# The prologue of a gated-linear-attention layer on one core: low-rank product and first unit begin with 288 tokens

## The chip, the cores and the metric

The kernel runs on one core of a Trainium2 chip. The metric is device microseconds of one execution. Three runs of the kernel before gave a median of 1057.85 us (1057.68 to 1058.1).

## What is computed

One decoder layer on 512 prompt tokens and 64 sample tokens (8 sequences of 8), 576 tokens of 1024 features. The layer normalizes x (RMS norm with a weight per feature), multiplies it by one wide input matrix, runs two gated linear recurrences (GLA and HGRN2) over slices of the product, merges them, projects them out, and runs a SwiGLU feed-forward network.

```python
def rms_norm(x, w):
    y = xf * lax.rsqrt(jnp.mean(xf * xf, axis=-1, keepdims=True) + EPS)
    return (y * w.astype(jnp.float32)).astype(x.dtype)
...
    proj = h @ w_in_l
    (gq, gk, gv, gg, glr, hq, hf, hi, hg, ga, gb) = jnp.split(proj, split_points, axis=-1)
    log_a = jax.nn.log_sigmoid((glr @ w_lr2_l + b_lr_l).astype(jnp.float32)) / GLA_TAU
...
            h = x + rms_norm(m, norm_mix_post[l])
            f = swiglu(rms_norm(h, norm_ffn_pre[l]), w_ffn_in[l], w_ffn_out[l])
            return h + rms_norm(f, norm_ffn_post[l])
```

The change touches only what happens to x before and during the first two products with `w_in`: those with the 16 columns `glr` and with the first 128 columns of `hf`.

## The kernel before

Every large product runs on TensorE in three passes over operands split in two: a value is a rounded main part (`x_hi`, `w_hi_t`) and a rest (`x_lo`, `w_lo_t`), and the passes are lo times hi, hi times lo and hi times hi. ScalarE makes main parts (a copy that rounds), VectorE makes rests (a subtraction). x is wanted with features on the 128 partitions, so each tile of 128 tokens is turned by 8 transposes of 128 by 128 on TensorE into PSUM, whence ScalarE and VectorE take main part and rest.

The tokens are five tiles: four of 128 (tiles 0 to 3) and one of 64 (tile 4, the sample tokens). The projections use two halves of 288 tokens (`HT`), so that the first half is tiles 0, 1 and the first 32 tokens of tile 2. Every engine has its program written out by hand, with semaphores between them; nothing is reordered.

The prologue, by engine:

- SyncE (SP, lines 433 to 441) issues the loads: the norm weight (`gain`, 4 KB), the five x tiles, the weights of the low-rank product (unit 0) and of the first unit (unit 1), 512 KB each, and then eight small ones. Later loads of weights wait for the splits of earlier ones.
- ScalarE (from line 555) loads its table, then for each tile takes squares and their sum (line 562), Ln (564) and Exp (566), which gives the inverse root; two tiles later it makes the main part of a turned tile (line 570). Then come the split of unit 2's weights (line 273, a helper) and the copy of the low-rank result.
- VectorE (from line 773) multiplies the identity with the norm weight into eight diagonal blocks (line 776), scales each tile by its inverse root and by the weight rows that stand in PSUM (line 783), and two tiles later subtracts for the rest (line 788). The rests are counted on the semaphore `x_lo_s`.
- TensorE (from line 1025) makes the weight rows by two matmuls of ones and the diagonal blocks (line 1029), turns the tiles (line 1039) with four dummy matmuls of ones and ones ahead of tiles 3 and 4 (line 1036), then makes the low-rank product for both halves (line 1046, 32 passes) and goes into the units: `unit_passes` (line 287) makes 48 passes of 288 columns for each.
- GpSimd (POOL, from line 472) splits the weights of units 0 and 1 into main part and rest, after which it builds masks (line 485 on) and, once all tiles are turned, loads states and copies the sample tokens into `x_both`.

The turned tiles go in turn to PSUM banks 0 and 1, 2 and 3, 4 and 5; the weight rows stand in banks 6 and 7; the low-rank product goes to banks 4 and 5, unit 1 to banks 2 and 3. These lines set the order on TensorE:

```python
        for c in range(NT):
            n = tok(c)
            if c >= 3:
                pe.wait_ge(x_lo_s, c - 2)
                for _ in range(4):
                    nc.tensor.matmul(ps[:, 3 * (c - 3), 0:P], ones[:, :], ones[:, :], start=True, stop=True)
            pe.wait_ge(scaled, c + 1)
            for k in range(KT):
                m = nc.tensor.transpose(turned_x(c)[:, k, :], xt[c][0:n, k * P:(k + 1) * P], ident[0:n, 0:n])
            m.then_inc(turned, 1)
        pe.wait_ge(w_lo, 2)
        for q in range(2):
            pe.wait_ge(x_lo_s, 3 if q == 0 else NT)
```

Of the kernel before, what the change touches and what calls it, by code (L numbers as in the profile page):

```python
# [63 lines left out]
V_BANK = {0: 2, 1: 3, 4: 4, 2: 0, 3: 1}  # L64
UB = 1 + G * NU
# [80 lines left out]
def build(nc, x_prompt, x_sample, state_gla, state_hgrn, norm_mix_pre, norm_mix_post, norm_ffn_pre,  # L146
# [53 lines left out]
    gain_diag = sem("gain_diag")  # L200
# [139 lines left out]
    gains = O[:, :, :].rearrange("p a b -> p (a b)")[:, 0:D].rearrange("p (k n) -> p k n", k=KT)  # L340
# [3 lines left out]
    def turned_x(c):  # L344
        return ps[:, 2 * (c % 3):2 * (c % 3) + 2, :].rearrange("p a b -> p (a b)").rearrange("p (k t) -> p k t", k=KT)[:, :, 0:tok(c)]

    def tokens(c):
        return slice(c * P, c * P + tok(c))

    square = v_t[:, :, :].rearrange("p a b -> p (a b)")[:, 0:D]  # L350
# [80 lines left out]
    @block.sync  # L431
    def _(sp):
        sp.dma_start(gain[:, 0, :], norm_mix_pre).then_inc(gain_in, 16)
        for c in range(NT):
            sp.dma_start(xt[c][0:tok(c), :], xp_v[c] if c < NC else xs_v).then_inc(x_in[c], 16)
        load_unit(sp, 0, win_v[:, :, GLR:GLR + P])
        load_unit(sp, 1, win_v[:, :, UNITS[0][0]:UNITS[0][0] + P])
        for t, v in ((gain[:, 1, :], hgrn_lb),
                     (onm[:, 0:2], gla_onorm), (onm[:, 2:3], hgrn_onorm), (blr4[:, :], gla_b_lr),
                     *((wlr4[i * GR:(i + 1) * GR, :], gla_w_lr2.rearrange("o r d -> (o r) d")) for i in range(4))):  # L440
            sp.dma_start(t, v).then_inc(small, 16)
        for j in range(G):
            for n, (col, width, t) in enumerate(UNITS):
                if j == 0 and n == 0:
                    continue
                u = j * NU + n + 1
                sp.wait_ge(w_lo, u)
                if col == "v":
                    load_values(sp, u, j, t)
                else:  # L450
                    first = j * width + col + t * P
                    load_unit(sp, u, win_v[:, :, first:first + P])
        for u in range(UB, UB + 5):
            sp.wait_ge(w_lo, u)
            load_out(sp, u)

    @block.gpsimd
    def _(pool):
# [84 lines left out]
        pool.wait_ge(x_hi_s, NT)  # L543
        nc.gpsimd.tensor_copy(x_both[:, :, 0:TS], x_hi[:, :, TP:T].bitcast(F32)).then_inc(both_s, 1)
        pool.wait_ge(x_lo_s, NT)
# [8 lines left out]
    def _(act):  # L554
        act.preload_act_table_set("natural_log_exp_and_others")

        act.wait_ge(setup, SETUP)
        for i in range(NT + 2):
            if i < NT:
                n = tok(i)  # L560
                act.wait_ge(x_in[i], 16)
                act.activation(square[0:n, :], xt[i][0:n, :], ACT.Square, accum_out=stat[0:n, 0, i:i + 1])
                act.drain()
                act.activation(stat[0:n, 1, i:i + 1], stat[0:n, 0, i:i + 1], ACT.Ln, scale=1.0 / D, bias=eps_c[0:n, :])
                act.drain()
                act.activation(stat[0:n, 1, i:i + 1], stat[0:n, 1, i:i + 1], ACT.Exp, scale=-0.5).then_inc(squared, 1)
            if i >= 2:
                c = i - 2
                act.wait_ge(turned, c + 1)
                act.activation(x_hi[:, :, tokens(c)], turned_x(c), ACT.Copy).then_inc(x_hi_s, 1)  # L570
# [193 lines left out]
    def _(dve):  # L764
# [9 lines left out]
        dve.wait_ge(consts, 5)  # L774
        dve.wait_ge(gain_in, 16)
# [3 lines left out]
        for i in range(NT + 2):  # L779
            if i < NT:  # L780
                n = tok(i)
                dve.wait_ge(squared, i + 1)
                dve.scalar_tensor_tensor(xt[i][0:n, :], xt[i][0:n, :], stat[0:n, 1, i:i + 1], gain_rows[0:n, :],
                                         ALU.mult, ALU.mult).then_inc(scaled, 1)
            if i >= 2:
                c = i - 2
                dve.wait_ge(x_hi_s, c + 1)
                dve.tensor_tensor(x_lo[:, :, tokens(c)], turned_x(c), x_hi[:, :, tokens(c)].bitcast(F32), ALU.subtract).then_inc(x_lo_s, 1)
# [236 lines left out]
    def _(pe):  # L1025
        pe.wait_ge(gain_diag, 1)
        pe.wait_ge(consts, 5)
        for k in range(2):
            m = nc.tensor.matmul(gain_rows[:, k * HALF:(k + 1) * HALF], ones[:, :], gains[:, 4 * k:4 * k + 4, :], start=True, stop=True)
        m.then_inc(gain_row, 1)  # L1030
        for c in range(NT):
            n = tok(c)
            if c >= 3:
                pe.wait_ge(x_lo_s, c - 2)
                for _ in range(4):
                    nc.tensor.matmul(ps[:, 3 * (c - 3), 0:P], ones[:, :], ones[:, :], start=True, stop=True)
# [4 lines left out]
        pe.wait_ge(w_lo, 2)  # L1041
        for q in range(2):
            pe.wait_ge(x_lo_s, 3 if q == 0 else NT)
# [4 lines left out]
        m.then_inc(unit_done, 1)  # L1048
# [134 lines left out]
        for j, n in SLOTS:  # L1183
            if j < G and V0 <= n < GATE0:
                value_unit(j, n - V0)
            elif j < G:
# [4 lines left out]
            elif n < 3:  # L1191
# [810 lines left out]
```

## Time and profile before

| | us |
|---|---|
| median of three runs | 1057.85 |
| the profiled execution | 1056.84 |
| its span, first to last instruction | 1055.1 |
| TensorE busy (matmuls) | 1040.6 (99%) |
| VectorE busy | 664.8 (63%) |
| ScalarE busy | 468.8 (44%) |
| GpSimd busy | 66.6 (6%) |
| first low-rank pass | 18.06 |
| first pass of unit 2 | 28.61 |

Times within the span are counted from its start. "SPq" and "POOLq" are instructions that issue a load or store; the load itself runs on the 16 DMA engines. A row of the timeline is a start, a duration, the engine, the line, the operation with output and inputs, and how many such instructions are merged into the row; in brackets stands the idle time before it and what ended it. Matmul rows overlap, so the distance of two starts says what one costs, and an f32 matmul has two records.

### The profile page before, as it was taken

How to read it: one execution, taken by the hardware profiler on the slowest of the kernel's cores; microseconds unless marked ns; L12 is line 12 of the kernel's file. 1: busy time of each engine (PE TensorE's matmuls, PEld its weight loads, DVE VectorE, ACT ScalarE, POOL GpSimd, SP SyncE). 2: the span in 40 equal slices, each digit the busy share in tenths (PEclk: the TensorE clock that was granted, in tenths of full speed). 3: DMA queues.
4: the chain of work that ended last, by engine and by line, in shares of the span. 5: the costliest groups of instructions: out<-in, count | busy, mean ns of one | idle time of the engine just before them, and what ended most of it. 6: DMA issues, size and time to landing. Idle time of an engine off the chain costs nothing.

```text
span 1055.1 us, 24326 instructions
## 1 busy us (share of the span) xinstructions
PE 1040.6 (99%) x10648; PEld 962.3 (91%) x10648; DVE 664.8 (63%) x974; ACT 468.8 (44%) x727; POOL 66.6 (6%) x86
## 2 busy tenths in 40 slices
PE   7999999999999999999999999999999999999997
PEld 5989999989999899999899878999999999888886
DVE  6266625676526756356765478888888888744544
ACT  6433344722445333446225547644444434633532
POOL 5200002100004000031000000000000000000000
PEclk9999999999999999999999999999999999999999
DMA  6522223622216332136232192133243242422212
GB/s 195 162 80 81 64 69 101 198 64 75 73 48 204 97 82 81 52 111 190 62 82 70 52 319 61 41 99 102 81 111 90 81 120 61 140 80 80 82 58 90
DMA packets 130777, 105.25 MB, mean 100 GB/s; under 512 B 4272, under 2 KB 115888, under 8 KB 130672
## 3 DMA queue, kind: packets, MB, share of 16 engines
q1 hardware_dynamic: 125808, 85.88, 28.3%
q0 software_dynamic: 4864, 17.83, 5.6%
q8 instruction: 84, 1.38, 0.5%
q14 instruction: 21, 0.17, 0.1%
HBM read 91.89 MB, written 11.80 MB: 98 GB/s over the span
## 4 chain that ended last, share of the span: by engine, by line
PE 94%; DVE 2%; ACT 1%; DMA 1%; ACTq 1%; issue 0%; DVEq 0%; SPq 0%
PE ps L287 34%; PE ps L1911 23%; PE ps L1935 13%; PE ps L1178 10%; PE ps L396 3%; PE ps L1080 2%; PE ps L1111 2%; PE ps L1101 1%; PE ps L1113 1%; PE ps L1118 1%; PE ps L1094 1%; PE ps L1150 1%; DVE h_t L937 1%; PE ps L1076 1%; PE ps L1138 0%; PE ps L1064 0%
## 5 line engine op out<-in xcount | busy, mean ns | idle before, releaser
L273 ACT ACTIVATE w_hi_t<-w_raw_t 128x1024 fp32r<-128x1024 f32 x73 | 77.2, 1058 | 302.1 <-PE ps L287 217.8
L287 PE MATMUL ps<-x_hi,w_lo_t 128*128 128x288 f32 x896 | 195.6, 300 | 0.0
L277 DVE TENSOR_TENSOR w_lo_t<-w_raw_t,w_hi_t 128x1024 fp32r<-128x1024 f32 x73 | 89.7, 1229 | 168.0 <-ACT w_hi_t L273 167.6
L287 PE MATMUL ps<-x_hi,w_hi_t 128*128 128x288 f32 x896 | 191.5, 295 | 0.0
L287 PE MATMUL ps<-x_lo,w_hi_t 128*128 128x288 f32 x896 | 191.0, 295 | 0.0
L287 PEld LDWEIGHTS ps<-x_hi,w_lo_t 128*128 128x128 f32 x896 | 143.0, 188 | 4.4 <-issue 2.5
L287 PEld LDWEIGHTS ps<-x_lo,w_hi_t 128*128 128x128 f32 x896 | 143.8, 188 | 0.0
L287 PEld LDWEIGHTS ps<-x_hi,w_hi_t 128*128 128x128 f32 x896 | 143.8, 188 | 0.0
L1911 PE MATMUL ps<-x_hi,w_lo_t 128*128 128x288 f32 x276 | 81.4, 295 | 0.6 <-issue 0.6
L1911 PE MATMUL ps<-x_lo,w_hi_t 128*128 128x288 f32 x276 | 81.3, 295 | 0.0
L1911 PE MATMUL ps<-x_hi,w_hi_t 128*128 128x288 f32 x276 | 81.3, 295 | 0.0
L1482 ACT ACTIVATE w_hi_t<-merged 128x1024 fp32r<-128x1024 f32 x35 | 37.0, 1057 | 57.4 <-PE ps L1911 57.4
L858 DVE TENSOR_TENSOR Q<-Q,B 128x768 f32<-128x768 f32 (+1 forms) x24 | 23.8, 992 | 58.8 <-PE ps L1080 23.8
L1935 PE MATMUL ps<-w_hi_t,x_hi 128*128 128x512 f32 x180 | 57.2, 390 | 0.0
L1911 PEld LDWEIGHTS ps<-x_hi,w_lo_t 128*128 128x128 f32 x276 | 51.8, 188 | 1.0 <-issue 1.0
L1722 DVE TENSOR_TENSOR work<-work,ps 128x288 f32<-128x288 f32 x100 | 45.1, 451 | 10.8 <-PE ps L1911 7.2
L1911 PEld LDWEIGHTS ps<-x_hi,w_hi_t 128*128 128x128 f32 x276 | 51.9, 188 | 0.0
L1911 PEld LDWEIGHTS ps<-x_lo,w_hi_t 128*128 128x128 f32 x276 | 51.8, 188 | 0.0
L1178 PE MATMUL ps<-w_lo_t,x_hi 128*128 128x512 f32 x128 | 51.3, 401 | 0.0
L1178 PE MATMUL ps<-w_hi_t,x_hi 128*128 128x512 f32 x128 | 50.0, 390 | 0.0
L1178 PE MATMUL ps<-w_hi_t,x_lo 128*128 128x512 f32 x128 | 49.8, 389 | 0.0
L1613 DVE TENSOR_TENSOR w_lo_t<-merged,w_hi_t 128x1024 fp32r<-128x1024 f32 x36 | 44.0, 1224 | 8.6 <-ACT w_hi_t L1482 8.6
(345 smaller groups left out, 2252.5 us busy)
## 6 DMA issues: line engine op xcount, KB each, us to landing
w_raw_t<-in_w_in_dram SPq DMA_DIRECT2D x57, 512.0 KB, 3.8
merged<-in_w_ffn_in_dram SPq DMA_DIRECT2D x22, 512.0 KB, 5.2
w_raw_t<-in_w_ffn_in_dram SPq DMA_DIRECT2D x22, 512.0 KB, 4.6
w_raw_t<-in_w_ffn_out_dram SPq DMA_DIRECT2D x22, 512.0 KB, 3.7
w_raw_t<-in_w_in_dram SPq DMA_DIRECT2D x32, 256.0 KB, 3.8
h_t<-in_x_prompt_dram SPq DMA_DIRECT2D x8, 512.0 KB, 5.0
h_t<-in_state_gla_dram POOLq DMA_DIRECT2D x4, 1024.0 KB, 6.4
h_t<-in_state_hgrn_dram POOLq DMA_DIRECT2D x8, 512.0 KB, 7.8
```

Source lines behind the costliest of these rows:

```text
L273: nc.scalar.activation(w_hi_t[:, u % NSPL, 0:nk, :], w_raw_t[:, u % NRAW, 0:nk, :], ACT.Copy).then_inc(w_hi, 1)
L277: nc.vector.tensor_tensor(w_lo_t[:, u % NSPL, 0:nk, :], w_raw_t[:, u % NRAW, 0:nk, :], w_hi_t[:, u % NSPL, 0:nk, :].bitcast(F32), ALU.subt ...
L287: m = nc.tensor.matmul(out[:, q, :], w[:, u % NSPL, k, :], x(k, q), start=first and i == 0, stop=last and i == len(todo) - 1)
L396: ins = pe.matmul(out_bank(half, c), x[:, k, cols], w[:, kk, :], start=first and i == 0, stop=last and i == len(todo) - 1, skip_group_chec ...
L858: dve.tensor_tensor(qf, qf, first.broadcast_to(shape), ALU.mult)
L1080: m = nc.tensor.matmul(s[t:t + STRIP, o + t // 2:o + (t + STRIP) // 2], K[:, h, c * C + t:c * C + t + STRIP], second(Q[:, h, c * C + t:c * ...
L1178: m = nc.tensor.matmul(ps[:, V_BANK[c], :], x, w, start=q == 0 and t == 0, stop=q == 3 and t == len(todo) - 1)
L1482: act.activation(group(i, g, True), group_raw(i, g), ACT.Copy).then_inc(g_hi, 1)
L1613: dve.tensor_tensor(group(i, g, False), group_raw(i, g), group(i, g, True).bitcast(F32), ALU.subtract).then_inc(first_lo if (i, g) in FIRS ...
L1722: return dve.tensor_tensor(out, term, bank(i, m), ALU.add)
L1911: ins = nc.tensor.matmul(bank(i, m), w[:, k0 + k, :], xx[:, k, :], start=(k == 0 and n == 0 and m in STARTS), stop=(k == 3 and n == 2), sk ...
L1935: m = nc.tensor.matmul(f_bank(half, t), x, w, start=first and i == 0, stop=last and i == len(todo) - 1)
```

## The change

The norm weight is loaded on ScalarE's queue, and the x tiles are issued in a row, with the weights of unit 0 after tile 2 and those of unit 1 after tile 3. The weight rows are made by eight f32 transposes of a broadcast column of the norm weight; VectorE's product with the identity is gone. VectorE makes the sum of squares of tile 1 by itself, and ScalarE does one Ln and one Exp for tiles 1 and 2 together. Tile 2 is taken in two parts, 32 tokens for the first half and 96 for the second, so that there are six main parts and six rests. TensorE runs twelve dummy matmuls ahead of tile 0, four after the first rest, then the low-rank product of the first half, tile 3's transposes, unit 1 of the first half with tile 4's transposes in its middle, the low-rank product of the second half and unit 1 of the second half. The PSUM banks of the turned tiles are now 0, 4, 2, 0 and 6.

```diff
+X_BANK = (0, 4, 2, 0, 6)
+X_PARTS = ((0, 0, P), (1, 0, P), (2, 0, HT - 2 * P), (2, HT - 2 * P, P), (3, 0, P), (4, 0, TS))
+NX = len(X_PARTS)
+FIRST_X = 3
...
     def _(sp):
-        sp.dma_start(gain[:, 0, :], norm_mix_pre).then_inc(gain_in, 16)
         for c in range(NT):
+            if c == 3:
+                load_unit(sp, 0, win_v[:, :, GLR:GLR + P])
+            if c == NC:
+                load_unit(sp, 1, win_v[:, :, UNITS[0][0]:UNITS[0][0] + P])
             sp.dma_start(xt[c][0:tok(c), :], xp_v[c] if c < NC else xs_v).then_inc(x_in[c], 16)
-        load_unit(sp, 0, win_v[:, :, GLR:GLR + P])
-        load_unit(sp, 1, win_v[:, :, UNITS[0][0]:UNITS[0][0] + P])
...
-        pool.wait_ge(x_hi_s, NT)
+        pool.wait_ge(x_hi_s, NX)
...
     def _(act):
+        act.dma_start(gain[:, 0, :], norm_mix_pre).then_inc(gain_in, 16)
         act.preload_act_table_set("natural_log_exp_and_others")
...
+        def square_sum(c):
+            n = tok(c)
+            act.wait_ge(x_in[c], 16)
+            act.activation(square[0:n, :], xt[c][0:n, :], ACT.Square, accum_out=stat[0:n, 0, c:c + 1])
+
+        def inverse_root(c0, c1):
+            n = tok(c0)
+            act.drain()
+            act.activation(stat[0:n, 1, c0:c1], stat[0:n, 0, c0:c1], ACT.Ln, scale=1.0 / D, bias=eps_c[0:n, :])
+            act.drain()
+            act.activation(stat[0:n, 1, c0:c1], stat[0:n, 1, c0:c1], ACT.Exp, scale=-0.5).then_inc(squared, c1 - c0)
+
+        def main_part(i):
+            act.wait_ge(turned, X_PARTS[i][0] + 1)
+            act.activation(x_hi[:, :, x_cols(i)], x_turned(i), ACT.Copy).then_inc(x_hi_s, 1)
+
+        square_sum(0)
+        inverse_root(0, 1)
+        square_sum(2)
+        act.wait_ge(sum_1, 1)
+        inverse_root(1, 3)
+        main_part(0)
+        main_part(1)
+        main_part(2)
+        square_sum(3)
+        inverse_root(3, 4)
+        act.wait_ge(x_lo_s, FIRST_X)
+        main_part(3)
+        square_sum(NC)
+        inverse_root(NC, NT)
+        main_part(4)
+        main_part(5)
...
-        dve.tensor_tensor(gains, ident[:, :].rearrange("p (o n) -> p o n", o=1).broadcast_to([P, KT, P]),
-                          gain[:, 0, :].rearrange("p (k o) -> p k o", o=1).broadcast_to([P, KT, P]), ALU.mult).then_inc(gain_diag, 1)
...
+        dve.wait_ge(x_in[1], 16)
+        dve.drain()
+        dve.scalar_tensor_tensor(square_1, xt[1], 1.0, xt[1], ALU.mult, ALU.mult, accum_out=stat[:, 0, 1:2]).then_inc(sum_1, 1)
         dve.wait_ge(gain_row, 1)
+        scale_x(0)
+        scale_x(1)
+        scale_x(2)
+        rest_part(0)
+        rest_part(1)
+        rest_part(2)
+        scale_x(3)
+        rest_part(3)
+        scale_x(NC)
+        rest_part(4)
+        rest_part(5)
...
     def _(pe):
-        pe.wait_ge(gain_diag, 1)
+        pe.wait_ge(gain_in, 16)
         pe.wait_ge(consts, 5)
-        for k in range(2):
-            m = nc.tensor.matmul(gain_rows[:, k * HALF:(k + 1) * HALF], ones[:, :], gains[:, 4 * k:4 * k + 4, :], start=True, stop=True)
+        for k in range(KT):
+            m = nc.tensor.transpose(gain_rows[:, k * P:(k + 1) * P], gain[:, 0, k:k + 1].broadcast_to([P, P]), ident[:, :])
         m.then_inc(gain_row, 1)
...
+        def first_unit(q):
+            for k in range(KT):
+                if q == 0 and k == KT // 2:
+                    turn_x(NC)
+                for n, (w, x) in enumerate(((w_lo_t, xh), (w_hi_t, xl), (w_hi_t, xh))):
+                    m = nc.tensor.matmul(proj(1)[:, q, :], w[:, 1, k, :], x(k, q), start=k == 0 and n == 0, stop=k == KT - 1 and n == 2)
+            return m
+
+        for _ in range(12):
+            nc.tensor.matmul(ps[:, 0, 0:P], ones[:, :], ones[:, :], start=True, stop=True)
+        turn_x(0)
+        turn_x(1)
+        turn_x(2)
+        pe.wait_ge(x_lo_s, 1)
+        for _ in range(4):
+            nc.tensor.matmul(ps[:, 0, 0:P], ones[:, :], ones[:, :], start=True, stop=True)
+        pe.wait_ge(w_lo, 2)
+        pe.wait_ge(x_lo_s, FIRST_X)
+        low_rank(0)
+        turn_x(3)
+        pe.wait_ge(x_lo_s, FIRST_X + 1)
+        pe.wait_ge(w_lo, 3)
+        first_unit(0)
+        pe.wait_ge(x_lo_s, NX)
+        low_rank(1).then_inc(unit_done, 1)
+        first_unit(1).then_inc(unit_done, 1)
```

`low_rank(q)`, `turn_x(c)`, `scale_x(c)` and `rest_part(i)` hold the bodies of the old loops for one half, one tile or one part; the general loop over units now begins with unit 2.

## Rows read from the trace of the kernel before

**Rows 1.** The page, busy time of each engine: us, share of the span, instructions.

```profile
PE 1040.6 (99%) x10648; PEld 962.3 (91%) x10648; DVE 664.8 (63%) x974; ACT 468.8 (44%) x727; POOL 66.6 (6%) x86
```

**Rows 2.** Waits of TensorE from 27 us on: total us, times, longest us.

```profile
PE ps L1911 <- issue: 0.6, 1, 0.6
...
PE ps L1911 <- DVE work L1722: 0.2, 1, 0.2
```

**Rows 3.** Chain of work of the first 40 us: start us, us, what.

```profile
1.26 3.83 DMA h_t<-in_x_prompt_dram
...
16.78 1.14 DVE x_lo L788
17.92 0.14 issue
18.06 4.48 PE ps L1046 x32
```

**Rows 4.** Timeline of TensorE in the prologue and at the start of unit 2.

```profile
4.01 3.43 PE L1029 MATMUL ps<-O,ones 128*128 128x512 f32 x4 [4.01 <-DVE O L776]
8.82 1.10 PE L1039 MATMUL ps<-ident,h_t 128*128 128x128 f32 x8 [1.38 <-DVE h_t L783]
...
11.67 1.09 PE L1039 MATMUL ps<-ident,h_t 128*128 128x128 f32 x8 [0.57 <-DVE h_t L783]
12.81 1.16 PE L1036 MATMUL ps<-ones 128*128 128x128 f32 x8
...
16.84 0.71 PE L1039 MATMUL ps<-ident,h_t 64*128 64x64 f32 x8 [0.28 <-DVE h_t L783]
...
28.61 0.42 PE L287 MATMUL ps<-x_hi,w_lo_t 128*128 128x288 f32 x2
```

**Rows 5.** Timeline of SyncE's queue: issues of loads.

```profile
0.81 0.39 SPq L433 DMA_DIRECT2D gain<-in_norm_mix_pre_dram  x1
1.26 1.84 SPq L435 DMA_DIRECT2D h_t<-in_x_prompt_dram  x4
```

**Rows 6.** Windows: us, PE, PEld, DVE, ACT, POOL busy (count), PEclk, DMA share, GB/s.

```profile
4.00:5.00 1.00, 0.99 (x1) 0.50 (x2) 0.00 (x0) 0.00 (x0) 0.00 (x0) 1.00 1.02 414
```

**Rows 7.** Timeline of GpSimd: splits of the weights of units 0 and 1.

```profile
13.90 0.40 POOL L477 CAST w_hi_t<-w_hi_t 128x256 fp32r<-128x256 f32 x1
14.24 1.04 POOL L479 CAST w_hi_t<-w_raw_t 128x1024 fp32r<-128x1024 f32 x1
15.37 2.37 POOL L481 TENSOR_TENSOR w_lo_t<-w_raw_t,w_hi_t 128x1024 fp32r<-128x1024 f32 x1
```

**Rows 8.** Timeline of VectorE in the prologue.

```profile
2.73 1.23 DVE L776 TENSOR_TENSOR O<-ident,gain 128x1024 f32<-128x1024 f32 x1 [1.73 <-DMA gain<-in_norm_mix_pre_dram]
7.48 2.47 DVE L783 SCALAR_TENSOR_TENSOR h_t<-h_t,stat,ps 128x1024 f32<-128x1024 f32 x2 [3.53 <-PE ps L1029]
10.34 1.28 DVE L783 SCALAR_TENSOR_TENSOR h_t<-h_t,stat,ps 128x1024 f32<-128x1024 f32 x1 [0.38 <-ACT stat L566]
```

**Rows 9.** Timeline of ScalarE in the prologue: square of tile 0 and its Exp.

```profile
5.18 1.06 ACT L562 ACTIVATE v_t<-h_t 128x1024 f32<-128x1024 f32 x1 [3.09 <-DMA h_t<-in_x_prompt_dram]
...
6.76 0.20 ACT L566 ACTIVATE stat<-stat 128x1 f32<-128x1 f32 x1
```

**Rows 10.** Issues of loads to 20 us: count, KB each, median us to landing.

```profile
gain<-in_norm_mix_pre_dram SPq DMA_DIRECT2D x1, 4.0 KB, 1.8
```

**Rows 11.** Groups by shape: busy us, mean ns of one, idle us before.

```profile
L1140 PE MATMUL ps<-Q,ones 128*128 128x288 f32 x8 | 2.2, 419 | 0.5 <-DVE h_t L937 0.5
L788 DVE TENSOR_TENSOR x_lo<-ps,x_hi 128x1024 fp32r<-128x1024 f32 x4 | 4.8, 1212 | 0.0
L788 DVE TENSOR_TENSOR x_lo<-ps,x_hi 128x512 fp32r<-128x512 f32 x1 | 0.7, 673 | 0.0
L822 DVE SCALAR_TENSOR_TENSOR B<-Z,T 128x1728 f32<-128x1728 f32 x1 | 2.0, 1951 | 0.0
L570 ACT ACTIVATE x_hi<-ps 128x1024 fp32r<-128x1024 f32 x4 | 3.9, 1005 | 0.0
```

More of the change, by code:

```diff
@@ L199, in build @@
     gain_in = sem("gain_in")
-    gain_diag = sem("gain_diag")
+    sum_1 = sem("sum_1")
     gain_row = sem("gain_row")
@@ L339, in build @@
     xt = [h_t[:, c, :] for c in range(NT)]
-    gains = O[:, :, :].rearrange("p a b -> p (a b)")[:, 0:D].rearrange("p (k n) -> p k n", k=KT)
     gain_rows = ps[:, 6:8, :].rearrange("p a b -> p (a b)")
@@ L554, in _ @@
     def _(act):
+        act.dma_start(gain[:, 0, :], norm_mix_pre).then_inc(gain_in, 16)
         act.preload_act_table_set("natural_log_exp_and_others")
         act.wait_ge(setup, SETUP)
[L558 to L570, printed above, removed]
+        def square_sum(c):
[27 more added lines that the diff above has]
+        main_part(5)
         act.wait_ge(small, 16 * 8)
@@ L773, in _, with scale_x, rest_part @@
         dve.drain().then_inc(merged_s, 1)
-        dve.wait_ge(consts, 5)
-        dve.wait_ge(gain_in, 16)
-        dve.tensor_tensor(gains, ident[:, :].rearrange("p (o n) -> p o n", o=1).broadcast_to([P, KT, P]),
-                          gain[:, 0, :].rearrange("p (k o) -> p k o", o=1).broadcast_to([P, KT, P]), ALU.mult).then_inc(gain_diag, 1)
-        dve.wait_ge(gain_row, 1)
[L779 to L788, printed above, removed]
+        def scale_x(c):
+            n = tok(c)
+            dve.wait_ge(squared, c + 1)
+            dve.scalar_tensor_tensor(xt[c][0:n, :], xt[c][0:n, :], stat[0:n, 1, c:c + 1], gain_rows[0:n, :],
+                                     ALU.mult, ALU.mult).then_inc(scaled, 1)
+        def rest_part(i):
+            dve.wait_ge(x_hi_s, i + 1)
+            dve.tensor_tensor(x_lo[:, :, x_cols(i)], x_turned(i), x_hi[:, :, x_cols(i)].bitcast(F32), ALU.subtract).then_inc(x_lo_s, 1)
+        dve.wait_ge(x_in[1], 16)
+        dve.drain()
+        dve.scalar_tensor_tensor(square_1, xt[1], 1.0, xt[1], ALU.mult, ALU.mult, accum_out=stat[:, 0, 1:2]).then_inc(sum_1, 1)
+        dve.wait_ge(gain_row, 1)
+        scale_x(0)
[9 more added lines that the diff above has]
+        rest_part(5)
         dve.wait_ge(small, 16 * 8)
@@ L1025, in _, with turn_x @@
     def _(pe):
-        pe.wait_ge(gain_diag, 1)
+        pe.wait_ge(gain_in, 16)
         pe.wait_ge(consts, 5)
-        for k in range(2):
-            m = nc.tensor.matmul(gain_rows[:, k * HALF:(k + 1) * HALF], ones[:, :], gains[:, 4 * k:4 * k + 4, :], start=True, stop=True)
+        for k in range(KT):
+            m = nc.tensor.transpose(gain_rows[:, k * P:(k + 1) * P], gain[:, 0, k:k + 1].broadcast_to([P, P]), ident[:, :])
         m.then_inc(gain_row, 1)
-        for c in range(NT):
+        def turn_x(c):
             n = tok(c)
[L1033 to L1036, printed above, removed]
             pe.wait_ge(scaled, c + 1)
@@ L1040, in _, with low_rank @@
             m.then_inc(turned, 1)
-        pe.wait_ge(w_lo, 2)
-        for q in range(2):
-            pe.wait_ge(x_lo_s, 3 if q == 0 else NT)
+        def low_rank(q):
             for k in range(KT):
@@ L1185, in _ @@
                 value_unit(j, n - V0)
-            elif j < G:
+            elif 0 < j < G or j == 0 and n > 0:
                 u = j * NU + n + 1
@@ L1190, in _ @@
                 unit_passes(u, proj(u), xh, xl).then_inc(unit_done, 1)
-            elif n < 3:
+            elif j == G and n < 3:
                 pe.wait_ge(unit_free, UB)
```

12 lines of the change are left out of this document (9 added, 3 removed).

## The prediction

> **What bounds the kernel now.** I read the page's busy shares first: TensorE is busy for 1040.6 of 1055.1 us [rows 1]. The reader is to see that VectorE (63%) and ScalarE (44%) are far from the bound, so that only idle time of TensorE, or work put on it, can move the end. Next come the waits of TensorE from 27 us to the end: four, together 1.6 us, of which the longest and the shortest stand here [rows 2]. From the second unit on, then, the engine runs through, and a start that is earlier by so much should reach the end whole. Nearly all idle time lies in the prologue, and the chain of work of the first 40 us shows what makes it: the load of x tile 0, then ScalarE's squares one tile after another, the last scaling, the last x_lo subtraction, and only then, at 18.06, the low-rank product [rows 3]. From there the stream is dense to the second unit of the projection, whose first pass starts at 28.61 [rows 4]: 10.55 us for 32 low-rank passes and 48 passes of the first unit. Those 28.61 us are what the change is measured against.
>
> **Loads.** The gain's load leaves SP's queue, so x tile 0 is issued at 0.81 instead of 1.26 [rows 5]. It landed 3.83 us after its issue [rows 3], so now at 4.64. Tile bytes move at 414 GB/s [rows 6], 1.27 us for 512 KB: tile 1 lands at 5.91, tile 2 at 7.18. SP then issues the low-rank weights, tile 3, the first unit's weights and tile 4. Of tiles 3 and 4 the first is wanted at 13.1 and the second at 15.6 (below); together with both weight loads all of it was in by 14.24 before, when GpSimd took up the second one [rows 7], and the queue starts 0.45 us sooner, so I cost the new order at nothing; were either later than it is wanted, the lateness would be added to the last part of the prologue. The low-rank weights were ready at 14.30 and the first unit's at 17.74 [rows 7]; both now go ahead of x bytes that they followed, so both come earlier by the queue's 0.45 us at least, and neither is the later of the two things that its reader waits for (14.3 and 17.7 below). The small loads behind them are read after 20 us on either side.
>
> **Norm weight.** Removed are VectorE's product of gain and identity (1.23 us, from 2.73) and two matmuls (3.43 us, 4.01 to 7.44) [rows 4, 8]. They held up the first scaling, which began at 7.48 though tile 0's statistic was ready at 6.96 [rows 8, 9]. Added are one load on ScalarE's queue and eight transposes. The load takes 1.8 us from issue [rows 10]; issued at about 0.8 it lands at 2.6 and TensorE starts at 2.7. The table load behind it on ScalarE (1.28 us) is over long before 4.64. Eight transposes took 1.10 us [rows 4], but that is at the full rate. The first two matmuls, 3.43 us in 4 records of 512 columns, need 1.68 ns a column, while f32 matmuls late in the kernel need 2.2 us for 8 records of 288, 0.95 ns a column [rows 4, 11]: the first work ran at or near the lower of the two levels (1.2 GHz), although the clock column reads 1.00 there [rows 6]. So I double the transposes to 2.2 us: gain rows stand at 4.9, between 3.8 and 4.9. That is before the first scaling wants them (7.2), so only what comes next on the same queue counts.
>
> **Twelve dummy matmuls** stand ahead of tile 0's transposes. Four took 1.16 us [rows 4], so twelve take 3.5 us at the full level and up to 7.0 at the lower one. Before, the work up to 7.44 was slow and the eight transposes at 8.82 were at full rate; so I take four of the dummies slow and eight at the full rate, 2.3 + 2.3 = 4.6 us, and tile 0's transposes start at 9.5, with 8.4 and 11.9 as ends.
>
> **Tiles 0 to 2.** Tile 0's statistic needs 1.78 us from the start of its square (5.18 to 6.96) [rows 9]: now 6.5. VectorE squares tile 1 itself: a scalar_tensor_tensor with two f32 inputs in SBUF took 1.95 us for 1728 elements, a scaling 1.28 for 1024 [rows 8, 11], so 1.2 to 1.3 us plus up to 0.2 to read the sum: 6.0 to 7.3. The cover is ScalarE's square of tile 2, 7.27 on, whose joint Ln and Exp end at 9.05; only a square later than 8.4 would be felt. Both waits that this adds have much behind them: VectorE's for tile 1 holds the first scaling (7.3 instead of 6.5, still ahead of 9.5), ScalarE's for the sum holds Ln, Exp and every main part. The Trainium skill (Vector Engine (DVE) Microarchitecture Reference, section Points that are easy to get wrong) warns that this form with two non-bf16 sources halves throughput. By that rule the square would end near 8.5 and the low-rank product start some 0.2 us later; the 1.13 ns an element of the row with two such sources does not show it.
>
> Then VectorE is the path: scalings of tiles 1 and 2 from 9.1 at a spacing of 1.19 (2.47 us for two) [rows 8], to 11.5; the rests of tiles 0 and 1 at 1.21 each; the rest of 32 columns of tile 2 (256 elements) 0.4, from 0.67 for 512 and 1.21 for 1024 [rows 11]. That ends at 14.15, and with the 0.14 us of issue that the old chain shows [rows 3] the low-rank product could start at 14.3. It holds if tile 0's rest isn't late at 11.5: its transposes (1.1) and its main part on ScalarE (1.01) [rows 4, 11] must start by 9.3. My 9.5 is 0.2 later, and every later start is felt in full: 14.5.
>
> **Tiles 3 and 4** move into the dense stream, where their transposes now cost TensorE time: 1.09 and 0.71 us [rows 4]. Their cover: ScalarE squares tile 3 from 13.1, VectorE scales it by 16.2, and the first low-rank half (16 passes, 2.1 us) ends at 16.6; with tile 3's transposes the first unit starts at 17.7. ScalarE squares tile 4 from 15.6, after the rest of tile 2's main part; it is scaled by 18.7 and wanted 12 passes later, at 19.3. Its rest ends near 21.2; the second low-rank half wants it at 21.6, a slack of 0.4 us, the thinnest of all, and what is missing there would be TensorE idle one for one. GpSimd's waits only count six parts instead of five tiles, and its copies for the value units are read tens of us later. The split of the second unit's weights moves behind the last main part, to about 20.5 to 23, and TensorE wants it at 27. The pass count is the same; that halves now go one after the other I cost at nothing, since a low-rank pass (4.48 us for 32, with the last one's tail) [rows 3] costs what a paired one does. I add 0.2 us for four changes between transposes and passes, between 0 and 0.4.
>
> **Sum.** 14.5 + 10.55 + 1.09 + 0.71 + 0.2 = 27.05 against 28.61: 1.56 us, I say 1.5. The profiled execution took 1056.84 us, 1.7 more than its span, and 1.0 less than the median of the runs, 1057.85; by its own time 1055.3, by the median 1056.4. Own range: dummies never felt and no cost of changes, 1.97 us gained (1055.9); all twelve slow, 16.9 + 12.35 + 0.2 = 29.4, 0.8 us lost (1058.6).
>
> **Rivals.** 0.2% (2.1 us) is about what a measurement of this kernel can tell from no change.
>
> A, more than 2.1 us gained (0.2): the bytes of x come sooner than I shift them, since no 4 KB load in small packets goes before them. Each 0.3 us that tile 2 gains moves VectorE's chain, and a clock that rises during the gain transposes lets tile 0 keep pace. With 0.3 us on top of the 1.97 of the sum's best case: 2.3 us, 1055.6. Against it: tile 2 to 14.15 is a chain of six measured durations.
>
> B, the front isn't early (0.18), the change not doing what it says. The gain is now on another queue beside the x tiles. If its packets are served among those of tile 0 it lands near 4.6, gain rows stand near 6.9, tile 0's transposes start at 11.5, the low-rank product at 16.5: 29.05, 0.4 us lost, 1058.3. Before, it was alone in front and landed in 1.8 us [rows 10], which says nothing of company. The other way to the same place is the clock: the dummies all slow, 1058.6. The Trainium skill (TensorE: Matmul & The Clock Gate, section Part 4: PE-mode transpose) says that the full clock doesn't engage for transposes. By it the eight gain transposes would do nothing for the clock, so say half of the dummies would be slow, 5.2 us; the start would be 10.1, and the gain 0.9. The trace speaks for neither: the clock had risen by 8.82, after matmuls alone.
>
> C, slower (0.1): TensorE falls to the lower level in the dense stream. Between the twelve dummies and the next four it has only three tiles' transposes, about 3 us with gaps, where the old order had four dummies ahead of tiles 3 and 4 each. A pass of 288 columns costs 0.13 us more at the lower level. 12 slow passes take back the 1.5 us, and from 28 on the kernel is over 2.1 us slower. All 80 slow: 1056.4 + 10.5 = 1066.9. Against it: from 7.44 to 12.81 the old order had only transposes and gaps, and the dummies at 12.81 were at full rate [rows 4].
>
> **How the numbers follow.** My forecast has 0.52, A 0.2, B 0.18, C 0.1. The forecast and B lie within 0.2%, so 0.7 for the same. The range takes in A's 1055.6 with 0.2 us for the runs' scatter, and B's 1058.3; beyond it lie C, part of A and the slowest dummies, 2 in 10.
>
> **What would show it.** Right: x tile 0's square at 4.7; gain transposes from 2.7, gain rows by 5; tile 0's transposes between 9 and 10; tile 1's scaling at 9.1; the first low-rank pass at 14.5; no wait of TensorE over 0.2 us from there to the second unit at 27.05; four waits with 1.6 us after it. Wrong: a wait of TensorE for the gain past 3.5; dummies at 0.58 us each throughout; a square of tile 1 that ends past 8.4; a wait ahead of the second low-rank half; passes at 0.26 us; a second unit that starts early while later waits grow.

## The result, and the profile after

The changed kernel took 1060.47 us (median of 20 executions, 1056.39 to 1062.11) against 1057.43 us for the kernel before (20 executions, 1056.71 to 1058.22): ratio 1.0023, 95% interval 1.0016 to 1.0031. It is slower by 2.4 us on that ratio and by 3.0 on the medians, outside my range, and the other way than forecast. Its executions fall into two groups, 6 from 1056.39 to 1057.68 and 14 from 1059.14 to 1062.11, with nothing between. The kernel before shows no such thing. The profiled execution (1060.37 us, span 1058.6) is one of the 14.

The upper group is itself in two parts. Five executions from 1059.14 to 1060.57 us, the profiled one among them, had a mean granted clock of TensorE of 0.999 or 1.0; the nine from 1061.27 to 1062.11 had 0.997 or 0.998. Their medians are 2.9 and 4.4 us above that of the lower group (1057.3). None of the nine was profiled.

TensorE in the timeline of the changed kernel (start, duration, count; in brackets the idle time before and what ended it):

```profile
4.90 1.97 PE L1071 MATMUL ps<-ident,gain 128*128 128x128 f32 x8 [4.90 <-DMA gain<-in_norm_mix_pre_dram]
6.66 4.92 PE L1097 MATMUL ps<-ones 128*128 128x128 f32 x24
11.42 2.78 PE L1078 MATMUL ps<-ident,h_t 128*128 128x128 f32 x24
16.38 0.37 PE L1084 MATMUL ps<-x_lo,w_hi_t 128*128 128x288 f32 x1 [0.40 <-DVE x_lo L814]
...
164.82 0.30 PE L1186 MATMUL ps<-As,v_t 128*32 128x64 f32 x3 [0.36 <-issue]
```

These answer to [rows 4]. The weight rows start at 4.90, where I had 2.7; tile 0's transposes at 11.42 instead of 9.5; the low-rank product at 16.38 instead of 14.5. Tile 0 was scaled by 8.43 (VectorE's first L809, 7.16 + 1.27), so for 3 us its transposes waited for nothing but the twelve dummies ahead of them. With the two moved sets of transposes unit 2 starts at 28.77 against 28.61: the prologue gained nothing. The waits of TensorE from 27 us on (total, times, longest; the five longest of seven), against the four of [rows 2]:

```profile
PE ps L291 <- ACT Z L625: 1.6, 1, 1.6
PE ps L1976 <- issue: 0.6, 1, 0.6
PE ps L1205 <- DVE h_t L979: 0.5, 1, 0.5
PE ps L1913 <- DVE a L1714: 0.4, 1, 0.4
PE ps L1186 <- issue: 0.4, 1, 0.4
```

The first, fourth and fifth are new; "issue" stands where TensorE waited for nothing that the profile shows. Laid beside the kernel before, matmul by matmul, TensorE is 0.15 us behind at 28.6, 2.26 at 41.2, 2.76 at 178, 2.87 at 278, 3.21 at 453 and 3.55 at 653, and it stays there. So 2.1 us are lost from 28.6 to 41.2 (most versions without the wait below lose 0.3 there, too), 0.8 at two places near 162 and 439, 0.35 near 652. The chain of work of the first 60 us (start, duration, what) tells the first:

```profile
0.80 4.06 DMA gain<-in_norm_mix_pre_dram
...
22.35 1.06 ACT w_hi_t L277
...
23.50 1.24 DVE w_lo_t L281
...
24.75 10.44 DMA w_raw_t<-in_w_in_dram
...
36.18 0.64 ACT Z L625
36.82 0.04 issue
36.86 6.65 PE ps L291 x48
```

The reader is to see a load of 512 KB that takes 10.44 us. It brings unit 4's weights. ScalarE, in order, splits them before it copies unit 1's result out of PSUM (L625), and unit 3 needs the banks that unit 1 had. GpSimd's timeline shows what shares the DMA engines with it:

```profile
23.41 1.06 POOL L520 DMA_DIRECT2D h_t<-in_state_gla_dram  x1
24.46 1.76 POOL L522 DMA_DIRECT2D h_t<-in_state_hgrn_dram  x2
```

2 MB of states, the first half issued 1.3 us ahead of it. Before, unit 4's load went out at 20.80 and was in after 4.2 us; the states went out at 27.14. Now the states come 3.7 us sooner, since GpSimd got its weights sooner, and unit 4's load 4 us later, since it waits for the split of unit 2.

### The profile page after: what moved, and what is told of

Read it like the earlier page. It is cut to its first block, busy times and chain, and to the rows that moved or that the text cites. A ratio compares the mean times of both kernels' runs of the same rounds, so it can differ in the third digit from the quotient of the medians.

```text
span 1058.6 us, 24364 instructions
## 1 busy us (share of the span) xinstructions
PE 1043.2 (99%) x10668; PEld 967.3 (91%) x10668; DVE 665.7 (63%) x976; ACT 467.4 (44%) x724; POOL 63.5 (6%) x86
## 4 chain that ended last, share of the span: by engine, by line
PE 92%; DVE 3%; ACT 2%; DMA 2%; issue 1%; DVEq 0%; ACTq 0%
PE ps L291 33%; PE ps L1976 23%; PE ps L2000 13%; PE ps L1243 10%; PE ps L1145 2%; PE ps L1176 1%; PE ps L1166 1%; PE ps L1178 1%; PE ps L405 1%; DMA w_raw_t<-in_w_in_dram 1%; PE ps L1183 1%; PE ps L1159 1%; PE ps L1215 1%; DVE h_t L979 1%; PE ps L1141 1%
## 5 line engine op out<-in xcount | busy, mean ns | idle before, releaser
L291 PE MATMUL ps<-x_hi,w_lo_t 128*128 128x288 f32 x880 | 192.5, 300 | 1.6 <-ACT Z L625 1.6
L291 PE MATMUL ps<-x_hi,w_hi_t 128*128 128x288 f32 x880 | 188.2, 295 | 0.0
L291 PE MATMUL ps<-x_lo,w_hi_t 128*128 128x288 f32 x880 | 187.7, 295 | 0.0
L291 PEld LDWEIGHTS ps<-x_hi,w_lo_t 128*128 128x128 f32 x880 | 140.5, 188 | 6.2 <-issue 2.5
L291 PEld LDWEIGHTS ps<-x_lo,w_hi_t 128*128 128x128 f32 x880 | 141.3, 188 | 0.0
L291 PEld LDWEIGHTS ps<-x_hi,w_hi_t 128*128 128x128 f32 x880 | 141.3, 188 | 0.0
L1976 PE MATMUL ps<-x_hi,w_lo_t 128*128 128x288 f32 x276 | 81.4, 295 | 0.6 <-issue 0.6
L1976 PE MATMUL ps<-x_lo,w_hi_t 128*128 128x288 f32 x276 | 81.3, 295 | 0.0
L1976 PE MATMUL ps<-x_hi,w_hi_t 128*128 128x288 f32 x276 | 81.3, 295 | 0.0
L1976 PEld LDWEIGHTS ps<-x_hi,w_lo_t 128*128 128x128 f32 x276 | 51.8, 188 | 1.0 <-issue 1.0
L1976 PEld LDWEIGHTS ps<-x_hi,w_hi_t 128*128 128x128 f32 x276 | 51.9, 188 | 0.0
L1976 PEld LDWEIGHTS ps<-x_lo,w_hi_t 128*128 128x128 f32 x276 | 51.8, 188 | 0.0
```

The lines of the kernel that those rows point to most:

```text
L291: m = nc.tensor.matmul(out[:, q, :], w[:, u % NSPL, k, :], x(k, q), start=first and i == 0, stop=last and i == len(todo) - 1)
L1976: ins = nc.tensor.matmul(bank(i, m), w[:, k0 + k, :], xx[:, k, :], start=(k == 0 and n == 0 and m in STARTS), stop=(k == 3 and n == 2), sk ...
```

## The experiments

Three theories: (1) the collision of unit 4's load and the states makes the wait near 35 and the two groups; (2) the norm weight lands late because its small packets take turns with tile 0's; (3) the stalls near 162 and 439 come from the place of the instructions in TensorE's lengthened program. Each edit stands as a short diff, cut at "...", against the changed kernel unless the kernel before is named. Times are medians of 10 to 12 executions unless another number is given, and each ratio is to the kernel before.

**States later (theory 1).**

```diff
+        pool.wait_ge(w_lo, 5)
         load_states(0)
```

> The changed kernel, and GpSimd issues the state loads only once the rest of unit 3's weights is made, so behind the loads of units 4 and 5. Theory 1 (the load of unit 4's weights, issued at 24.75 and landed at 35.19, is slow because it shares the DMA engines with the 2 MB of states issued from 23.41, and this makes TensorE wait near 35): the load of unit 4 lands in about 4 us, the wait of 1.6 us goes, and so does the scatter of the changed kernel (1056.4 to 1062.1 in 20 runs); median near 1057.3, as before the change. Rival (the load is slow by its own descriptors or its place in SP's queue, or the slow executions come from elsewhere): the load still takes some 10 us, median 1060.

Median 1057.37 us (1055.97 to 1058.80, 11 executions), ratio 1.0000 (0.9991 to 1.0009). The states are issued at 28.96. Unit 4's load, issued at 23.64, is in after 4.0 us instead of 10.4:

```profile
w_raw_t<-in_w_in_dram SPq DMA_DIRECT2D x1, 512.0 KB, 4.0
```

The profile names no wait of TensorE from 28 to 600 us, and no execution is above 1058.8, where 14 of 20 were above 1059. Theory 1 holds for the wait and for the upper group as a whole. The median is that of the lower group, so without the collision the change is worth nothing either way: the rest of the 1.5 us is missing for other reasons.

**Split of unit 2 earlier (theory 1, the other side).**

```diff
         inverse_root(NC, NT)
+        act.wait_ge(w_raw[2 % NRAW], loaded(2))
+        act.wait_ge(w_lo, 3)
+        split_hi(2)
         main_part(4)
...
         scale_x(NC)
+        dve.wait_ge(w_hi, 3)
+        split_lo(2)
         rest_part(4)
```

> The changed kernel, but the split of unit 2's weights stands ahead of the last two main parts and rests instead of behind them. Theory 1 says that the load of unit 4 collides only because it waits for this split (24.73 in the changed kernel, 20.8 before): it is now issued near 21.3, ahead of the states at 23.4, lands before 28, and TensorE has no wait near 35; the second low-rank half may wait 0.2 us more for its rest; median 1057.3. Rival (it is the early states alone that count, wherever the weight load stands): a later load, that of unit 5, is slow in its place and TensorE waits as long one unit later, median 1060.

1057.19 us (1056.51 to 1058.15), ratio 0.9999 (0.9990 to 1.0008). Unit 4's load is issued at 19.82, the states at 24.34; no wait near 35. The later load of unit 5, behind the states, is slow too (ScalarE waits 6.78 us for it), but TensorE doesn't feel it. So either end of the collision can be moved.

**Norm weight first on SP's queue (theory 2).**

```diff
     def _(sp):
+        sp.dma_start(gain[:, 0, :], norm_mix_pre).then_inc(gain_in, 16)
...
     def _(act):
-        act.dma_start(gain[:, 0, :], norm_mix_pre).then_inc(gain_in, 16)
```

> The changed kernel, with the norm weight issued first on SP's queue again. Theory 2 (on ScalarE's queue its packets share the DMA engines with x tile 0 and so it lands at 4.86 instead of 2.63): it lands near 2.6, the eight gain transposes start at 2.7 instead of 4.90, all x tiles land 0.45 us later, the first low-rank pass comes 1.2 to 1.6 us sooner than 16.38, at about 15.0. Rival (every load of ScalarE's queue or the first one of the kernel is slow by itself, or the start of the transposes is not what tile 0 waits for): the first low-rank pass stays at 16.4 or comes later. In the end, with the collision as it is, 1056 to 1060.

1057.02 us (1056.23 to 1057.78), ratio 0.9996 (0.9987 to 1.0005). TensorE's timeline:

```profile
2.45 1.97 PE L1071 MATMUL ps<-ident,gain 128*128 128x128 f32 x8 [2.45 <-DMA gain<-in_norm_mix_pre_dram]
4.21 3.52 PE L1097 MATMUL ps<-ones 128*128 128x128 f32 x24
9.05 1.09 PE L1078 MATMUL ps<-ident,h_t 128*128 128x128 f32 x8 [1.31 <-DVE h_t L809]
...
14.88 0.37 PE L1084 MATMUL ps<-x_lo,w_hi_t 128*128 128x288 f32 x1 [0.40 <-DVE x_lo L814]
```

The low-rank product starts 1.5 us sooner than in the changed kernel, though the x tiles land some 0.5 us later (tile 0 at 5.15 instead of 4.63). Tile 0 now waits for its scaling; I had had it wait for the dummies, until 9.5. With the prologue quicker, unit 4's load (23.26) is ahead of the states (25.04) again, and the upper group is gone.

**The kernel before, with only that load moved (theory 2).** The same two lines, the other way round, in the kernel before.

> The kernel before, with only the norm weight's load moved to ScalarE's queue. Theory 2: the load lands at 4.8 instead of 2.6, the product with the identity, the two matmuls and the first scaling start 2.2 us later (9.7 instead of 7.5), x tile 0 lands 0.45 us sooner, and as ScalarE's squares set the end of the old chain only part of it is felt: the first low-rank pass between 18.0 and 20.0, median 1057 to 1059. Rival (queue of no importance): the load lands at 2.6, the first low-rank pass 0.4 us sooner, 17.6, median 1057.0.

1059.48 us (1058.69 to 1060.14), ratio 1.0017 (1.0008 to 1.0026). The weight lands at 4.62 instead of 2.63. The first matmul starts at 6.00 instead of 4.01; unit 2 starts 2.00 us late, the end is 2.2 late. The move of one 4 KB load costs 2 us by itself.

**The load alone.**

```diff
     def _(sp):
+        sp.wait_ge(gain_in, 16)
         for c in range(NT):
```

> The changed kernel, but SP issues its first x tile only when the norm weight has landed; everything else starts later by that much. It asks why the weight lands 4.1 us after its issue on ScalarE's queue. Theory 2 (its 32-byte packets take turns with tile 0's of 4 KB on each DMA engine): alone it lands 1.8 us after the issue, near 2.6. Rival (the queue of ScalarE, or the first load that it issues, is slow by itself): still near 4.8. The time as a whole is of no use here.

One execution only (1058.36 us, of no use as a time). Issues of the first 6 us, count, KB, us to landing: first the changed kernel, then this one.

```profile
gain<-in_norm_mix_pre_dram ACTq DMA_DIRECT2D x1, 4.0 KB, 4.1
```

```profile
gain<-in_norm_mix_pre_dram ACTq DMA_DIRECT2D x1, 4.0 KB, 1.6
```

The queue of ScalarE isn't slow; the company is. In the changed kernel the 128 packets of 32 bytes start from 2.31 to 4.20, and 141 packets of 4 KB start between the first and the last of them; first on SP's queue they started from 1.80 to 2.06 with none between. The Trainium skill (DMA: Bandwidth & Descriptors, section Queues, rings and completion order) says that an engine takes turns between the queues that have work; the packet times agree, with about one large packet for each small one.

**The kernel before, with its states early (theory 1).** `load_states(0)` stands behind the splits of units 0 and 1, with its wait for `turned`, instead of behind the masks.

> The kernel before, with GpSimd's three state loads issued as soon as all tiles are turned (about 17.7) instead of behind the masks (27.1). Unit 4's weights are issued at 20.8, behind them. Theory 1: that load takes 8 to 10 us instead of 4 and lands near 30, but TensorE needs it only by about 32, so no wait, or one under 0.5 us, and the median stays at 1057.5. Rival (the load in the changed kernel was slow for a reason of its own): it lands in 4 us, by 25.

1057.49 us (1056.82 to 1058.28, 10 executions), ratio 1.0000 (0.9991 to 1.0009). The load of unit 4, issued at 21.55 behind the states at 18.60, is as slow as in the changed kernel. ScalarE's timeline, the split that waits for it:

```profile
32.03 1.06 ACT L273 ACTIVATE w_hi_t<-w_raw_t 128x1024 fp32r<-128x1024 f32 x1 [6.94 <-DMA w_raw_t<-in_w_in_dram]
```

21.55 to 32.0 is 10.5 us, and TensorE has no wait there. The same slow load costs nothing when it is issued 3 us sooner.

**Ten tiny matmuls in the kernel before (theory 3).**

```diff
         m.then_inc(gain_row, 1)
+        for _ in range(10):
+            nc.tensor.matmul(ps[:, 0, 0:8], ones[:, :], ones[:, 0:8], start=True, stop=True)
```

> The kernel before, with ten matmuls of 8 columns added in TensorE's idle time behind the weight rows (7.44 to 8.82); with two records and two weight loads each they add the 40 instructions by which the change lengthens TensorE's program, and nothing else. Theory 3 (the stalls of TensorE at the As products near 161 and 439 us and at the last turn near 652 us, 0.4 to 0.9 us in all, which no semaphore explains and which every changed kernel has, come from where the instructions now lie in the program): the same stalls appear, and the kernel is 0.3 to 1.0 us slower than before. Rival (they come from GpSimd's, VectorE's or the loads' new timing): no stall at these places, time within 0.2 us of before, plus what the ten cost if they reach into the first transposes (at most 0.5 us).

1061.73 us (1058.59 to 1062.33, 5 executions), ratio 1.0031 (1.0019 to 1.0043).

```profile
7.36 4.27 PE L1032 MATMUL ps<-ones 128*128 128x8 f32 x20
11.48 5.36 PE L1041 MATMUL ps<-ident,h_t 128*128 128x128 f32 x24
...
166.31 0.30 PE L1123 MATMUL ps<-As,v_t 128*32 128x64 f32 x3 [0.37 <-issue]
...
444.47 0.31 PE L1123 MATMUL ps<-As,v_t 128*32 128x64 f32 x5 [0.74 <-issue]
```

Two readings. The stalls appear at the same two places, in the middle of a burst of As products, with no semaphore between: the lag grows by 0.58 us at the first and 0.94 at the second. That is for theory 3. And what I didn't expect: the ten cost 4.3 us, and the transposes behind them stand 0.213 us apart instead of 0.11, the lower level. In the profiled execution unit 2 starts 3.4 us late, most of what is lost; the median is no measure of what the stalls cost.

What the stalls wait for can be told in part. The trace of every version has a queue of transfers that it calls "instruction" (packets, MB, and share of 16 engines, in this run):

```profile
q8 instruction: 84, 1.38, 0.6%
```

These are 84 packets of 16,384 bytes. This run and the changed kernel each have 21,667 records of TensorE, one packet for some 258. The two stalled instructions stand 7,425 records apart, which is 29 times 256 and one more. In the six traces in which a stall can be seen, nine stalls in all, they start 2.3 to 2.8 us after such a packet's start (166.31 after 163.72 and 444.47 after 441.71 here, 164.82 after 162.21 in the changed kernel). So the likely reading is that TensorE ran through a burst of short products faster than the next piece of its program came, and that 40 instructions more put the border between two pieces inside the burst. No run tests this reading by itself.

**The cures together, with 2 front dummies.** Weight first on SP's queue, split early, and

```diff
-        for _ in range(12):
+        for _ in range(2):
```

> The changed kernel with the norm weight first on SP's queue, the split of unit 2's weights ahead of the last two parts, and 2 instead of 12 dummy matmuls at the front, which brings TensorE's program to the length that it had before. If theories 1 to 3 hold and the front dummies are not needed: the first low-rank pass at 14.9 (if the transposes stay slow without the dummies, 0.22 us each, up to 15.8), no wait from 28 to 600 us, no stalls near 161, 439 and 652 us, 1055.9 to 1056.2 median, 1.3 to 1.5 us faster than before. If the dummies are needed to bring the clock up, passes of the low-rank half take 0.26 us and the kernel is slower by up to several us. If theory 3 is wrong: 1056.8.

1057.23 us (1056.56 to 1057.85), ratio 0.9995 (0.9987 to 1.0004). No stall at 162 or 439, the lag there grows by nothing. But it is 1 us slower than the 1055.9 to 1056.2 that I expected, and the front shows why:

```profile
4.21 1.06 PE L1097 MATMUL ps<-ones 128*128 128x128 f32 x4
9.11 5.60 PE L1078 MATMUL ps<-ident,h_t 128*128 128x128 f32 x24 [3.84 <-DVE h_t L809]
14.51 1.46 PE L1103 MATMUL ps<-ones 128*128 128x128 f32 x8
15.80 0.37 PE L1084 MATMUL ps<-x_lo,w_hi_t 128*128 128x288 f32 x1
```

The 24 transposes are at the lower level from first to last (0.213 us from one to the next, where 0.11 was seen at the upper), and the low-rank product comes at 15.80. They did not bring the clock up in 5.6 us: the distance falls to 0.11 only from 15.35 on, behind four of the next dummies' eight records. With the weight early and TensorE idle for 3.84 us behind two dummies, the other ten are needed.

**The cures with 12 dummies.** The same without the last diff.

> As the run before, but with all 12 front dummies. First low-rank pass at 14.9, no wait from 28 to 160 us; by theory 3 the stalls near 161, 439 and 652 us remain, and the median is 1056.8, between the run before (1056.0) and the kernel before (1057.4). Rival: no difference from the run before.

1056.96 us (1056.61 to 1057.40), ratio 0.9995 (0.9987 to 1.0004). The low-rank product starts at 14.87; both stalls are there again, 0.26 and 0.46 us of lag.

**The changed kernel with 2 dummies alone.**

> The changed kernel with 2 instead of 12 front dummies, nothing else. The weight still lands near 4.8, the gain transposes end at 6.7, so tile 0's transposes start with its scaling at 8.5 instead of 11.4 and the first low-rank pass comes at 14.4 to 15.3 instead of 16.4. Unit 2's split, unit 4's load with it, moves ahead of the states in every execution, so no wait near 35 us and no slow executions: by theory (twelve dummies at a clock that rises now sooner, now later decide who goes first) all runs below 1058, median 1056.1 to 1056.6. Rival (the scatter has another source): still about two runs in three above 1059.

1056.48 us median, ratio 0.9993 (0.9985 to 1.0002); ten of 12 executions lie from 1056.03 to 1056.66, the others at 1059.03 and 1060.71. The profiled one is one of the two: states at 23.07, unit 4's load at 23.75, a wait of 1.9 us. I had expected no slow execution; the groups are still there, with other shares (2 of 12 instead of 14 of 20). All three profiles with the wait have the states ahead, by 0.7 to 1.3 us, and the profiles with unit 4's load ahead have none, so the order of the two probably decides; no execution of a lower group was profiled.

This run also shows what the dummies cost behind a late weight. Tile 0's transposes start at 8.38, when the tile is scaled, instead of 11.42; they run at the lower level throughout, and yet the low-rank product starts at 15.09, 1.3 us sooner than in the profile of the changed kernel. Whether twelve dummies help or hurt depends on when the weight lands.

**The changed kernel, same dummy columns in fewer instructions (theory 3).**

```diff
-        for _ in range(12):
-            nc.tensor.matmul(ps[:, 0, 0:P], ones[:, :], ones[:, :], start=True, stop=True)
+        for _ in range(4):
+            nc.tensor.matmul(ps[:, 0, 0:3 * P], ones[:, :], ones[:, 0:1].broadcast_to([P, 3 * P]), start=True, stop=True)
```

and the four behind tile 2 as two of 256 columns.

> The changed kernel with the dummy columns in 40 instructions fewer (four matmuls of 384 and two of 256 columns), nothing else. Theory 3: no stall near 161 and 439 us, that near 652 us stays. The collision of unit 4's load with the states stays as it was, so executions fall into two groups: about 1056.5 and about 1060, each some 0.5 us below those of the changed kernel (1057.1 and 1061.4). Rival: both groups as in the changed kernel.

1057.98 us, ratio 1.0003 (0.9993 to 1.0013), 6 executions from 1055.47 to 1057.30 and 6 from 1058.66 to 1060.89: two groups again, with medians of 1056.1 and 1059.2 where those of the changed kernel are 1057.3 and 1061.4. No stall at 162 or 439; the wait near 35 (1.6 us) and the one near 652 (0.4 us) are left. Its two slowest executions (1060.36 and 1060.89) have a mean granted clock of 0.998, the other four of the upper group 0.999, as in the changed kernel.

**All of it.** Weight first on SP's queue, split early, and the wide dummies.

> As the run with the cures and 12 front dummies (first load of the weight on SP's queue, split of unit 2 ahead of the last two parts), but the dummy columns come in fewer instructions: four matmuls of 384 columns instead of twelve of 128, two of 256 instead of four, the same columns and 40 instructions fewer, so that TensorE's program is as long as before the change. Theory 3 (place of the instructions): first low-rank pass at 14.9 as there, no stalls near 161 and 439 us, median 1056.4, some 0.5 us below that run's 1056.96. Rival (the two dummies fewer in the other run acted in another way): the stalls stay and the median is 1057.0.

1055.90 us (1055.71 to 1056.73), ratio 0.9986 (0.9977 to 0.9994): by the medians of that call (1057.54 before) 1.6 us faster than the kernel before, and the only version whose interval excludes no difference on the fast side. The low-rank product starts at 14.74, unit 2 at 27.27 (my sum said 27.05), 1.3 us sooner than before, and 1.1 us of that reach the end of the profiled span. Its waits of TensorE past 27 us are the four of [rows 2]:

```profile
PE ps L1976 <- issue: 0.6, 1, 0.6
PE ps L1205 <- DVE h_t L979: 0.5, 1, 0.5
PE ps L405 <- DVE x_both L987: 0.3, 1, 0.3
PE ps L1976 <- DVE work L1787: 0.2, 1, 0.2
```

The runs side by side, in us of the profiled execution: first low-rank pass, issue of unit 4's weights and of the states, the wait near 35, the lag gained at 162 and 439 together.

| | low-rank | unit 4 | states | wait | 162 + 439 | median |
|---|---|---|---|---|---|---|
| before | 18.06 | 20.80 | 27.14 | 0 | 0 | 1057.43 |
| changed | 16.38 | 24.75 | 23.41 | 1.6 | 0.84 | 1060.47 |
| states later | 15.26 | 23.64 | 28.96 | 0 | 0.41 | 1057.37 |
| split earlier | 14.98 | 19.82 | 24.34 | 0 | 0.56 | 1057.19 |
| weight on SP | 14.88 | 23.26 | 25.04 | 0 | 0.58 | 1057.02 |
| both, 12 dummies | 14.87 | 20.20 | 25.15 | 0 | 0.72 | 1056.96 |
| both, 2 dummies | 15.80 | 21.64 | 25.51 | 0 | 0 | 1057.23 |
| changed, 2 dummies | 15.09 | 23.75 | 23.07 | 1.9 | 0 | 1056.48 |
| changed, wide | 15.76 | 24.13 | 23.01 | 1.6 | 0 | 1057.98 |
| both, wide | 14.74 | 20.07 | 24.56 | 0 | 0 | 1055.90 |

## Why the prediction was wrong

The step that turned the sign is the one on the second unit: "The split of the second unit's weights moves behind the last main part, to about 20.5 to 23, and TensorE wants it at 27". The time was nearly right (22.35 to 24.74) and the question too narrow. I asked who reads the split and not what its completion releases: SP's load of unit 4, which thereby went out at 24.75 instead of 20.80. Nor did I follow GpSimd: "its copies for the value units are read tens of us later" is true, but its 2 MB of loads come ahead of the copies and moved from 27.14 to 23.41. The states early in the kernel before, or the late split with the states held back, bring no wait; that the two cross costs 1.8 us in the profiled execution. Without the crossing there is no upper group. But its medians lie 2.9 and 4.4 us above the lower group, so the wait is not all of it: 1.5 us of the larger distance goes with the lower mean clock of the nine executions, and where in them TensorE was slow isn't known. (A lower mean by itself need cost nothing: the last 3 us of the profiled execution count as lower, and one execution of the version with both cures and 2 dummies had 0.996 at 1056.99 us.) None of my rivals named the crossing.

The second failed step is "issued at about 0.8 it lands at 2.6": 4.86. I took the time of the load when it was first and alone. Rival B had this and its mechanism. It put the low-rank product at 16.5 (16.38 came) and unit 2 at 29.05 (28.77 came). I gave it 0.18 because the row "says nothing of company"; the nearest answer, the packets of 4 KB that such a load has to stand among, could have been priced from 414 GB/s over 16 engines: 0.16 us a packet, eight turns, 1.3 of the 2.2 us that it came late.

The dummies were mis-sized with it. I took 0.29 us for one at the upper level and 0.58 at the lower; each has two records, and these start 0.11 and 0.213 us apart, so a dummy costs 0.22 or 0.43. I also took four of twelve at the lower level; in the profiled execution 20 of the 24 records were. The two errors nearly cancel, 4.92 us against the 4.6 that I took, which is luck. Rival B's other way, "the dummies all slow", thus nearly came, too. Behind a weight that lands at 4.86 they hold tile 0's transposes until 11.42.

Last, that the program had grown by 40 instructions on TensorE I didn't cost at all: 0.4 to 0.8 us in the profiles of the changed kernel and its cures, and about 1 us between the twins with and without them (1056.96 against 1055.90).

What held: VectorE's chain from tile 2's statistic to the low-rank product. With the weight on SP's queue it predicts 14.3 + 0.45 = 14.75, and 14.74 to 14.88 were measured. That the two agree to 0.1 us has some luck in it: the chain's own terms (11.5, twice 1.21, 0.4) add up to 14.32 and not to the 14.15 that I wrote, and the three rests took 2.69 us in a row, not 2.82. The square of tile 1 took 1.23 us and held nothing up. Tiles 3 and 4 cost what their transposes cost, and no wait arose before the second low-rank half. Rival A didn't occur. Rival C neither: all 80 passes ran at 0.13 us. The sum of 1.5 us was thus near for a kernel that has neither the collision, nor the late weight, nor the longer program. The last version is that kernel: 1.3 us at unit 2, 1.1 at the end of the profile, 1.6 by the medians.

Left open: why TensorE waits 0.35 us more near 652 in all versions that keep the split of unit 2 behind the last parts, and in none that have it ahead, when the stage lies 600 us later. Theory 3 is shown by twins (instructions added, stalls come; taken away, they go); that the stalls are waits for the next piece of the program is worked out from the packets' times and not tested. What decides in which group an execution falls is open, too. The moment at which the clock rises is a candidate: the same twelve dummies took 3.48 us in one profile and 4.92 in another, and every start behind them moves. But no execution of the lower group of the changed kernel was profiled, and none of its nine slowest.

## What to carry to other kernels

When work is moved on one engine, follow what each of its completions releases, on every queue, until the next buffer: a split that nobody reads for 4 us can hold back a load that then meets another engine's bulk transfer. A small load on a queue of its own isn't free of the queue beside it; put first on the busy queue, it cost the tiles 0.5 us and brought the product forward by 1.5. Where executions of a kernel fall into two groups, look for two events in the profile whose order is nearly a tie. And compare the distance of the groups with the wait that you found: here the wait is 1.8 us and the groups are 2.9 and 4.4 apart.

## What the hardware showed that was not expected

Transposes didn't bring TensorE's clock up. With 2 dummies at the front, 24 transposes in a row stayed at 0.22 us each for 5.6 us, and the passes behind the next dummies ran at full rate. The Trainium skill (TensorE: Matmul & The Clock Gate, section Part 4: PE-mode transpose) says that the full clock doesn't engage for transposes; these runs agree, though transposes that began at the upper level kept it (1.09 us for 8 at 9.05 and on). Behind the ten matmuls of 8 columns they were slow as well (5.36 us for 24).

Instructions cost by where they lie: 40 more at the start of a program of over 20,000 on TensorE put stalls of 0.2 to 0.9 us into two bursts of short matmuls 160 and 440 us later.
